# Hybrid DeltaNet and sparse-attention trunk: RMS norms whose reciprocal root is applied to the products, and reordered outer norms

## The chip, the cores and the metric

The kernel runs on one core of one Trainium2 chip. The metric is the device time of one execution in microseconds (us). Before the change it is 1827.06 us, the median of 3 runs (1824.49 to 1828.47).

## What is computed

Two decoder layers and a final norm on T = 320 tokens (256 of a prompt, 64 of eight sampled sequences) with D = 1024 features, in float32. Cut to what matters here:

```python
def rms_norm(x, w):
    xf = x.astype(jnp.float32)
    xf = xf * lax.rsqrt(jnp.mean(xf * xf, axis=-1, keepdims=True) + RMS_EPS)
    return xf.astype(x.dtype) * w
# gdn:  proj = rms_norm(x, norm_w) @ w_in; gated delta rule; x = x + o @ w_out
# ffn:  up = rms_norm(x, w) @ w_up; hidden = silu(conv(gate)) * up; x = x + hidden @ w_down
# nsa:  proj = rms_norm(x, norm_w) @ w_in; sparse attention; x = x + o @ w_out
# y = rms_norm(x, final_norm)
```

The order is gdn, ffn (first), nsa, ffn (second), final norm. The reciprocal root is one number per token, the weight one per feature.

## The kernel before

The tokens are kept turned: `xT` holds x as KD = 8 tiles of 128 features x 320 tokens. A projection is a row of *units*: gdn_in 24, gdn_out 8, ffn_up 22, ffn_down 8, nsa_in 10, nsa_out 4. A unit of gdn_in, ffn_up, nsa_in and nsa_out has two tiles of 128 output features, called lane 0 and lane 1 (in ffn_up the gate and the up half); a unit of the others has one, on lane 1. Each lane has two PSUM banks used in turn. For near-float32 results each operand is split in a high part and the rest, both in the rounded fp32r format: `high_part` on ScalarE (ACT, L496) and `low_part` on VectorE (DVE, L511) do this for the weights, and TensorE (PE) makes three products per tile (`three_products`, L535 to L537): 48 products for the two lanes of a unit with 8 feature tiles.

Weights arrive in a ring of RING = 4 slots, filled by SyncE's (SP) DMA queue in `stream`, which waits until PE is through with the unit that had the slot (`unit_done`). The engines run programs written out by hand for each stage and meet at barriers: each engine drains, raises `stage_closed` and waits until all four have.

A norm is made of these pieces. `square_tiles` (L363 to L367) lets ACT square each tile of x once the residual add of the stage before (`add_tile`, L1508, on DVE) has made it. `sum_of_squares` (L348 to L357) lets PE add them over features with 8 matmuls against a matrix of ones (L355). After a barrier `norm_stage` (L412 to L447) runs: ACT high part of unit 0, square root (L423), high part of unit 1; DVE low part of unit 0, reciprocal (L435), then for each of the 8 tiles the scaled x (L439), ACT's cast to the high part (L429) and DVE's low part (L444). PE then starts on unit 0. The start of the program has `pe_turns` (L369 to L383), which turns x, norm rows and convolution rows, and `copy_turned` (L385 to L400), which copies them out of PSUM and in between makes one square of all of x (L392). At the end `norm_stage` writes the normed x, `final_stage` (L2479 to L2510) turns it back in six groups, copies and stores it.

In `ffn_stage` (L1511) ACT takes the gate tile out of PSUM (L586, L587), makes the first tap of the convolution (L592), the next high part, silu (L615, L616) and the hidden high part (L1582); DVE makes the later taps (L610), the product of silu and up (L1619, which reads up from PSUM), the next low part and the hidden low part (L1623). PE also turns the last rows of each gate (L1556) into bank 4; ACT copies them out with `copy_rows` (L1586). In nsa_in ACT copies every tile out of PSUM, and POOL (GpSimd) issues loads in `pool_in`: attention tables, compressed keys `ckT` and values `cv`. In the rows stage POOL loads `w1_again` (L1896, 4 MB in two DMAs), which PE needs at L1831. The lines of such a program, as the second FFN's adds are:

```python
def add_tile(dve, name, j):
    dve.wait_ge(unit_done, UNITS[name][0] + j + 1)
    dve.tensor_tensor(xT[:, j, :], xT[:, j, :], bank(name, j, 1)[:, 0:T], ALU.add).then_inc(lane_free[1], 1)
```

## Time and profile before

| | |
|---|---|
| median of 3 runs | 1827.06 us |
| profiled execution | 1825.39 us, its span 1823.5 us |
| PE busy | 1638.0 us, 90% of the span |
| DVE busy | 865.5 us, 47% |
| ACT busy | 771.7 us, 42% |
| POOL busy | 195.6 us, 11% |
| DMA | 208.10 MB, mean 114 GB/s |
| gdn_in with its start, gates, core | 0 to 785 us |
| gdn_out, norm, ffn_up and ffn_down, first FFN | 785 to 1097 us |
| norm, nsa_in | 1097 to 1186 us |
| NSA rows, attention, nsa_out | 1186 to 1554 us |
| norm, second FFN | 1554 to 1802 us |
| final norm and stores | 1802 to 1823.5 us |

The page of the profile comes from one execution. Its share of busy time is a mean over stages of different kinds: where PE is the engine that never waits, work on other engines is free, and where PE idles, the chain that it waits for counts. So each boundary is looked at by itself, in the engines' timelines. PEclk is the clock that PE was granted, as a share of 2.4 GHz; 0.50 is 1.2 GHz.

### The profile page before, as it was taken

The numbers are of one execution on the slowest core, as the hardware profiler recorded it, in microseconds if no ns is written. First come the engines' busy times: TensorE is split into PE (matmuls) and PEld (weight loads), VectorE is DVE, ScalarE is ACT, GpSimd is POOL, SyncE is SP. The second block draws the span as 40 slices with busy tenths as digits, with TensorE's granted clock in tenths as the row PEclk, the third lists the DMA queues.
The fourth block names the chain that finished last, engine by engine and source line by source line (L and its number), as shares of the span: only waits on it lengthen the run. The fifth ranks groups of instructions, "written<-read, shape, count | busy, mean of one in ns | idle before, by whom it ended". The sixth has DMA issues, their size and how long they took to land. (4 is left out here: it accounts for less than half of the span.)

```text
span 1823.5 us, 37321 instructions
## 1 busy us (share of the span) xinstructions
PE 1638.0 (90%) x13536; PEld 1347.5 (74%) x13536; DVE 865.5 (47%) x1585; ACT 771.7 (42%) x1600; POOL 195.6 (11%) x396
## 2 busy tenths in 40 slices
PE   5999989999999999798999998977787777899997
PEld 4999756556655665487999997975555557799996
DVE  3875234444444344454555524224655543655632
ACT  3765233444234334433555414224444533555521
POOL 0331001011101110100000001021112100000000
PEclk7999979999989999888999998957778967999998
DMA  6445331321233122433555665344435313355640
GB/s 147 139 149 160 125 103 35 91 83 51 76 88 86 41 84 71 122 86 99 139 152 153 167 132 157 116 170 131 142 107 163 114 47 116 94 156 143 178 127 29
DMA packets 283161, 208.10 MB, mean 114 GB/s; under 512 B 29103, under 2 KB 274895, under 8 KB 282592
## 3 DMA queue, kind: packets, MB, share of 16 engines
q1 hardware_dynamic: 273750, 174.22, 34.2%
q0 software_dynamic: 9248, 31.80, 5.6%
q8 instruction: 79, 1.29, 0.3%
q14 instruction: 42, 0.34, 0.1%
q10 hardware_dynamic: 42, 0.44, 0.1%
HBM read 183.57 MB, written 22.85 MB: 113 GB/s over the span
## 5 line engine op out<-in xcount | busy, mean ns | idle before, releaser
L535 PE MATMUL psum<-h_rounded,weights_low 128*128 128x320 f32 x1248 | 395.5, 317 | 33.6 <-DVE h_low_ffn L444 16.7
L535 PEld LDWEIGHTS psum<-h_rounded,weights_low 128*128 128x128 f32 x1248 | 236.3, 189 | 40.2 <-issue 34.8
L997 PE MATMUL psum<-sbuf_resident 128*128 128x504 f32 x512 | 252.8, 609 | 0.0
L537 PE MATMUL psum<-h_rounded,weights_high_wide 128*128 128x320 f32 x704 | 220.2, 313 | 0.0
L536 PE MATMUL psum<-h_low_ffn,weights_high_wide 128*128 128x320 f32 x704 | 218.9, 311 | 0.0
L537 PE MATMUL psum<-h_rounded,weights_high 128*128 128x320 f32 x544 | 168.2, 309 | 0.0
L511 DVE TENSOR_TENSOR weights_low<-sbuf_resident,weights_high_wide 128x2048 fp32r<-128x2048 f32 (+1 forms) x60 | 149.8, 2499 | 16.5 <-ACT weights_high_wide L496 16.5
L610 DVE SCALAR_TENSOR_TENSOR sbuf_stages<-sbuf_stages,sbuf_resident 128x344 f32<-128x344 f32 (+1 forms) x184 | 105.5, 574 | 99.9 <-ACT sbuf_stages L592 96.1
L1030 ACT COPY sbuf_resident<-psum 64x256 f32<-64x256 f32 x256 | 93.8, 366 | 138.6 <-PE psum L990 136.0
L496 ACT CAST weights_high_wide<-sbuf_resident 128x2048 fp32r<-128x2048 f32 (+1 forms) x60 | 123.8, 2063 | 66.9 <-DMA sbuf_resident<-in_ffn_w_down_dram 60.1
L511 DVE TENSOR_TENSOR weights_low<-sbuf_resident,weights_high 128x2048 fp32r<-128x2048 f32 x46 | 105.3, 2293 | 74.5 <-ACT weights_high L496 74.5
L536 PEld LDWEIGHTS psum<-h_low_ffn,weights_high_wide 128*128 128x128 f32 x704 | 136.2, 194 | 0.0
L537 PEld LDWEIGHTS psum<-h_rounded,weights_high_wide 128*128 128x128 f32 x704 | 133.1, 189 | 0.0
L997 PEld LDWEIGHTS psum<-sbuf_resident 128*128 128x128 f32 x512 | 87.0, 194 | 54.1 <-issue 52.1
L536 PE MATMUL psum<-weights_low,weights_high 128*128 128x320 f32 x384 | 119.2, 310 | 0.0
L496 ACT CAST weights_high<-sbuf_resident 128x2048 fp32r<-128x2048 f32 x46 | 86.8, 1896 | 68.3 <-PE psum L537 36.9
L535 PE MATMUL psum<-hidden_high,weights_low 128*128 128x320 f32 x352 | 109.2, 310 | 0.0
L536 PE MATMUL psum<-hidden_low,weights_high_wide 128*128 128x320 f32 x352 | 108.9, 309 | 0.0
L537 PE MATMUL psum<-hidden_high,weights_high_wide 128*128 128x320 f32 x352 | 108.7, 309 | 0.0
L537 PEld LDWEIGHTS psum<-h_rounded,weights_high 128*128 128x128 f32 x544 | 104.2, 191 | 0.0
L586 ACT COPY sbuf_stages<-psum 128x256 f32<-128x256 f32 x76 | 28.3, 373 | 172.9 <-PE psum L537 171.1
L1508 DVE TENSOR_TENSOR sbuf_resident<-sbuf_resident,psum 128x320 f32<-128x320 f32 x24 | 11.7, 488 | 136.6 <-PE psum L537 136.6
(418 smaller groups left out, 3077.7 us busy)
## 6 DMA issues: line engine op xcount, KB each, us to landing
sbuf_resident<-in_ffn_w_up_dram SPq DMA_DIRECT2D x88, 512.0 KB, 4.8
sbuf_resident<-in_gdn_w_in_dram SPq DMA_DIRECT2D x48, 512.0 KB, 4.7
sbuf_resident<-in_ffn_w_down_dram SPq DMA_DIRECT2D x32, 704.0 KB, 5.8
sbuf_resident<-in_cache_nsa_kv_dram SPq DMA_DIRECT2D x256, 64.0 KB
sbuf_stages<-in_state_gdn_s_dram POOLq DMA_DIRECT2D x16, 512.0 KB, 5.5
out_gdn_s_sample_dram<-sbuf_stages SPq DMA_DIRECT2D x16, 512.0 KB, 3.7
sbuf_resident<-in_gdn_w_out_dram SPq DMA_DIRECT2D x16, 512.0 KB, 5.5
sbuf_stages<-in_cache_nsa_kv_dram POOLq DMA_DIRECT2D x64, 128.0 KB, 3.5
```

The source lines that it names most:

```text
L496: act.copy(dst[:, 0:kn * P], slot(w)[:, 0:kn * P]).then_inc(hi_done, 1)
L511: eng.tensor_tensor(ring_lo[w % RING][:, 0:kn * P], sl, hi[:, 0:kn * P], ALU.subtract).then_inc(lo_done, 1)
L535: pe.matmul(out, w_lo, x_hi_tile, start=first, stop=False)
L536: pe.matmul(out, w_hi, x_lo_tile, start=False, stop=False)
L537: return pe.matmul(out, w_hi, x_hi_tile, start=False, stop=last)
L586: act.copy(xp[:, hist:hist + TP], src[:, 0:TP])
L610: dve.scalar_tensor_tensor(out=y[:, 0:n_out], in0=xp[:, n:n + n_out], scalar=taps(n), in1=y[:, 0:n_out], op0=ALU.mult, op1=ALU.add).then_i ...
L997: last = pe.matmul(psum[:, H_BANK[t], 0:4 * NC2], w1[:, v, 8 * half + m, t * P:(t + 1) * P], blocks, start=(m == 0 and half == 0), stop=(m ...
L1030: last = act.copy(dst, src)
L1508: dve.tensor_tensor(xT[:, j, :], xT[:, j, :], bank(name, j, 1)[:, 0:T], ALU.add).then_inc(lane_free[1], 1)
```

## The change

The inner norms no longer make a normed x. During the residual adds of the stage before, ACT writes the high part of x times the weight and the squares, DVE the low part and the running sum of the squares. PE starts the next projection's lane 0 of unit 0 at once, then runs one ones-matmul on the sum, then lane 1. Root and reciprocal are made meanwhile, and the projections' results are multiplied by `rinv` where they leave PSUM: in ffn_up by `take_gate` and `take_up` on DVE (the product then reads SBUF twice), in nsa_in by DVE, which takes over all evictions from ACT; the 48 gate logits get an operation of their own. Six barriers become plain increments. High parts of ffn_up go to the narrow buffers. At the start unit 0's weights are loaded before the convolution rows, x is squared in three chunks of tokens, DVE adds the squares over tiles, one matmul sums them, and most turns come after it; there the normed x is still made. For the final norm, x times the weight is turned back in between the last down units, the sums come from three matmuls of one column, and the six copies to the output rows carry the reciprocal root. Because the final turns use bank 4, PE waits for ACT's last `copy_rows` ahead of the second ffn_down. The loads of `ckT` and `cv` move from nsa_in to the head of POOL's queue in the rows stage. The core of the diff:

```diff
+            for n in range(6):
+                turn(n)
+            pe.wait_ge(norm_rows_in, 16 * 4)
+            turn(6)
+            pe.wait_ge(dve_steps.sem, dve_steps.count("tile2"))
...
+            for c, cols in enumerate(CHUNKS):
+                copy_turn(act, 2 * c + 1)
+                act.wait_ge(dve_steps.sem, dve_steps.count(f"g{2 * c}"))
+                act.wait_ge(act_steps.sem, act_steps.count(f"g{2 * c + 1}"))
+                act.activation(hT[:, :, cols], xT[:, :, cols], ACT.Square).then_inc(act_steps.sem, act_steps.step(f"square{c}"))
+            act.wait_ge(S1["pe"].sem, S1["pe"].count("sum"))
+            act.activation(rinv, psum[:, SUM_BANK, 0:T], ACT.Sqrt, bias=eps_col, scale=1.0 / D).then_inc(act_steps.sem, act_steps.step("root"))
+            high_part(act, "gdn_in", 0, 0, KD * 2, free=True)
...
+            def dve_tile(self, dve, k):
+                dve.wait_ge(x_hi, SPLITS[self.units][0] + k + 1)
+                dve.scalar_tensor_tensor(out=self.low_rounded(k), in0=xT[:, k, :], scalar=self.weight(k), in1=hT_rounded[:, k, :],
+                                         op0=ALU.mult, op1=ALU.subtract).then_inc(x_lo, 1)
+                if k:
+                    self.add(dve, k)
...
+            def pe_sum(self, pe):
+                pe.wait_ge(self.dve_steps.sem, self.dve_steps.count(f"added{KD - 1}"))
+                pe.matmul(psum[:, SUM_BANK, 0:T], ones, rinv, start=True, stop=True).then_inc(self.pe_steps.sem, self.pe_steps.step("sum"))
...
+            def act_adding(self, act, kn):
+                n = UNITS[self.prev][1]
+                for j in range(n):
+                    if j + 3 < n:
+                        high_part(act, self.prev, 0, j + 3, kn)
+                    if self.units and j + 2 >= n:
+                        act.wait_ge(unit_done, UNITS[self.prev][0] + j + 1)
+                        high_part(act, self.units, 0, j + 2 - n, KD * 2)
+                    self.act_tile(act, j)
+
+            def dve_adding(self, dve, kn):
+                n = UNITS[self.prev][1]
+                for j in range(n):
+                    add_tile(dve, self.prev, j)
+                    if j + 3 < n:
+                        low_part(dve, self.prev, j + 3, kn)
+                    if j + 2 == n:
+                        low_part(dve, self.units, 0, KD * 2)
+                    self.dve_tile(dve, j)
+                low_part(dve, self.units, 1, KD * 2)
+
+            def pe_first_unit(self, pe, tile, high, low):
+                multiply_unit(pe, self.units, 0, 0, tile, high, low, KD, lanes=(0,), from_tile=0)
+                self.pe_sum(pe)
+                multiply_unit(pe, self.units, 0, 0, tile, high, low, KD, lanes=(1,))
...
+                    eng.wait_ge(rows_copied, len(ROWS) + 1)
+                    for j in range(8):
+                        multiply_unit(eng, down, 0, j, single_tile(NFT), lambda k: hidden_hi[:, k, :], lambda k: hidden_lo[:, k, :], NFT,
+                                      lanes=(1,), from_tile=NFT - 2 if j == 0 else None)
+                        if j:
+                            fin["pe_turn"](eng, j - 1)
...
                     eng.wait_ge(unit_done, product_count(up, 0, u, 1))
-                    eng.tensor_tensor(hid[:, u, :], sil[u % 2], bank(up, u, 1)[:, 0:T], ALU.mult).then_inc(lane_free[1], 1)
+                    eng.tensor_tensor(hid[:, u, :], bank(up, u, 1)[:, 0:T], rinv, ALU.mult).then_inc(lane_free[1], 1)
...
+                def take_gate(u):
+                    eng.wait_ge(half_done, product_count(up, 0, u, 0))
+                    if u >= 2:
+                        eng.wait_ge(tail_kept, u - 1)
+                    src, xp = bank(up, u, 0), xpf[u % 2]
+                    eng.tensor_tensor(xp[:, FP:FP + TP], src[:, 0:TP], rinv[:, 0:TP], ALU.mult)
+                    eng.tensor_tensor(padded(xp, FP)[:, :, FP:FP + TQ], seqs(src[:, TP:T]), seqs(rinv[:, TP:T]), ALU.mult).then_inc(lane_free[0], 1)
...
-                            ins_ = act.copy(kvT[:, 2 * (n - 4) + l, :], src)
...
+                            ins_ = dve.tensor_tensor(kvT[:, 2 * (n - 4) + l, :], src, rinv, ALU.mult)
                         ins_.then_inc(lane_free[l], 1)
-
...
+                dve.tensor_tensor(gates48, psum[0:48, 6, 0:T], rinv[0:48, :], ALU.mult).then_inc(gate_scaled, 1)
...
+                pool.dma_start(ckT, ck_dram).then_inc(cmp_in, 16)
+                pool.dma_start(cv, cv_dram).then_inc(cmp_in, 16)
...
+            def pe_turn(pe, k):
+                pe.wait_ge(x_hi, SPLITS["final"][0] + k + 1)
+                for tb in range(3):
+                    last = pe.transpose(psum[:, Y_BANK[2 * tb + k // 4], (k % 4) * P:(k % 4 + 1) * P], hT[:, k, y_rows[tb]], ident)
+                last.then_inc(s["pe"].sem, s["pe"].step(f"x{k}"))
...
-            sums_f0["pe"](pe)
-            pe.drain().then_inc(stage_closed, 1)
-            pe.wait_ge(stage_closed, 4 * 5)
+            pe.sem_inc(stage_closed, 1)
```

**DVE between gdn_out and the first ffn_up.** Before, from the last three residual adds (L1508): low part of unit 0, reciprocal, then scale and low part of each tile (the first of eight).

```order
L1508 TENSOR_TENSOR sbuf_resident<-sbuf_resident,psum 128x320 x3
L511 TENSOR_TENSOR weights_low_49<-sbuf_resident,weights_high_wide_57 128x2048
L435 RECIPROCAL sbuf_resident<-sbuf_resident 128x320
L439 SCALAR_TENSOR_TENSOR sbuf_stages<-sbuf_resident 128x320 x2
L444 SCALAR_TENSOR_TENSOR h_low_ffn_66<-sbuf_stages,h_rounded 128x320
L439 SCALAR_TENSOR_TENSOR sbuf_stages<-sbuf_resident 128x320
```

Of the change, from the last residual add (L1592) on: L488 is the low part of the weighted x, L479 the running sum, L597 low parts of weights, L1720 and L1721 the gate's eviction, L1713 the up half's.

```order
L1592 TENSOR_TENSOR sbuf_resident<-sbuf_resident,psum 128x320
L488 SCALAR_TENSOR_TENSOR weighted_x_low<-sbuf_resident,h_rounded 128x320
L479 TENSOR_TENSOR sbuf_resident<-sbuf_resident,sbuf_stages 128x320
L597 TENSOR_TENSOR weights_low_50<-sbuf_resident,weights_high_54 128x2048
L503 RECIPROCAL sbuf_resident<-sbuf_resident 128x320
L1720 TENSOR_TENSOR sbuf_stages<-psum,sbuf_resident 128x256
L1721 TENSOR_TENSOR sbuf_stages<-psum,sbuf_resident 128x8x8
L696 SCALAR_TENSOR_TENSOR sbuf_stages<-sbuf_stages,sbuf_resident 128x336 x2
L597 TENSOR_TENSOR weights_low_51<-sbuf_resident,weights_high_55 128x2048
L1713 TENSOR_TENSOR sbuf_stages<-psum,sbuf_resident 128x320
```

The work on the eight tiles has moved ahead of the last add, low part 0 lies before the rows shown, and the reciprocal has only the low part of unit 1 ahead of it and the first eviction behind it.

**PE between the second ffn_up and ffn_down,** before, with what each row waits for (L1556 turns the last rows of a gate):

```order
L537 MATMUL psum<-h_rounded,weights_high_wide_58 128x320
L1556 MATMUL psum<-sbuf_resident,sbuf_stages 18x128 [waits ffn1_rows_copied,ffn1_tail_kept]
L1556 MATMUL psum<-sbuf_resident,sbuf_stages 18x128 [waits ffn1_tail_kept]
L1502 UNCONDITIONAL_BRANCH [waits activations_low_part_done]
L535 MATMUL psum<-hidden_high,weights_low_51 128x320 [waits lane1_banks_free,weights_low_part_done]
```

and of the change (L1640 is that turn, L621 and L622 the products):

```order
L623 MATMUL psum<-h_rounded,weights_high_54 128x320
L1640 MATMUL psum<-sbuf_resident,sbuf_stages 18x128 [waits ffn1_rows_copied,ffn1_tail_kept]
L1640 MATMUL psum<-sbuf_resident,sbuf_stages 18x128 [waits ffn1_tail_kept]
L621 MATMUL psum<-hidden_high,weights_low_51 128x320 [waits lane1_banks_free,weights_low_part_done,ffn1_rows_copied]
L622 MATMUL psum<-hidden_low,weights_high_wide_59 128x320
```

The first down product has one more wait, `ffn1_rows_copied`.

**ACT at the same place,** before, from the last hidden high part:

```order
L1582 CAST hidden_high<-sbuf_stages 128x320 [waits lane1_banks_free]
L496 CAST weights_high_wide_60<-sbuf_resident 128x2816 [waits weights_in_slot3]
L1586 COPY sbuf_resident<-psum 18x256 [waits ffn1_tails_turned]
L496 CAST weights_high_wide_57<-sbuf_resident 128x2816 [waits unit_done,weights_in_slot0]
L496 CAST weights_high_wide_58<-sbuf_resident 128x2816 [waits unit_done,weights_in_slot1]
```

and of the change:

```order
L1674 CAST hidden_high<-sbuf_stages 128x320 [waits ffn1_product]
L582 CAST weights_high_wide_60<-sbuf_resident 128x2816 [waits weights_in_slot3]
L1678 COPY sbuf_resident<-psum 18x256 [waits ffn1_tails_turned]
L582 CAST weights_high_wide_57<-sbuf_resident 128x2816 [waits unit_done,weights_in_slot0]
L582 CAST weights_high_wide_58<-sbuf_resident 128x2816 [waits unit_done,weights_in_slot1]
L2669 ACTIVATE sbuf_resident<-sbuf_resident 128x320 [waits lane1_banks_free]
L472 ACTIVATE sbuf_resident<-sbuf_resident 128x320
```

The copy for which PE now waits (L1586, now L1678) keeps its place behind one wide cast; behind it the weighted copies and squares (L2669, L472) come in among the casts.

## Rows read from the trace of the kernel before

**Rows 1.** Windows: stretch, length, busy (count) by engine, PEclk, DMA share, GB/s

```profile
846.00:866.00 20.00, 11.81 (x52) 9.76 (x51) 14.35 (x21) 9.79 (x16) 1.68 (x4) 0.74 0.19 53
...
1576.00:1723.00 147.00, 147.00 (x1003) 145.86 (x1002) 87.10 (x104) 79.86 (x153) 9.61 (x62) 1.00 0.57 154
...
1802.00:1823.00 21.00, 8.51 (x38) 6.66 (x36) 8.01 (x12) 3.80 (x6) 1.64 (x3) 0.72 0.18 63
```

**Rows 2.** PE timeline, the first FFN's norm: start us, duration us, instruction

```profile
844.83 4.48 PE L355 MATMUL psum<-sbuf_resident 128*128 128x320 f32 x16
...
857.50 0.60 PE L535 MATMUL psum<-h_rounded,weights_low 128*128 128x320 f32 x1 [8.19 <-DVE h_low_ffn L444]
...
867.34 0.31 PE L535 MATMUL psum<-h_rounded,weights_low 128*128 128x320 f32 x1
```

**Rows 3.** PE timeline at the start of the program

```profile
8.59 4.39 PE L382 MATMUL psum<-sbuf_resident,sbuf_stages 128*128 128x128 f32 x24 [8.59 <-DMA sbuf_resident<-tables_dram]
...
47.12 0.31 PE L535 MATMUL psum<-h_rounded,weights_low 128*128 128x320 f32 x1
```

**Rows 4.** ACT timeline at the start

```profile
13.49 2.34 ACT L392 ACTIVATE sbuf_resident<-sbuf_resident 128x2560 f32<-128x2560 f32 x1
...
41.83 0.46 ACT L429 CAST h_rounded<-sbuf_resident 128x320 fp32r<-128x320 f32 x1 [0.41 <-DVE sbuf_resident L439]
```

**Rows 5.** ACT timeline in the NSA norm

```profile
1102.95 1.28 ACT L423 ACT_TABLE_LOAD   x1
1104.25 0.53 ACT L423 ACTIVATE sbuf_resident<-psum,sbuf_stages 128x320 f32<-128x320 f32 x1
```

**Rows 6.** DVE timeline in the first FFN's norm

```profile
853.60 2.15 DVE L435 RECIPROCAL sbuf_resident<-sbuf_resident 128x320 f32<-128x320 f32 x1
```

**Rows 7.** DVE timeline, one round of the first FFN's up-projection

```profile
917.68 0.49 DVE L1619 TENSOR_TENSOR sbuf_stages<-sbuf_stages,psum 128x320 f32<-128x320 f32 x1 [1.07 <-ACT sbuf_stages L616]
918.09 2.29 DVE L511 TENSOR_TENSOR weights_low<-sbuf_resident,weights_high_wide 128x2048 fp32r<-128x2048 f32 x1
920.29 0.48 DVE L1623 SCALAR_TENSOR_TENSOR hidden_low<-sbuf_stages,hidden_high 128x320 fp32r<-128x320 f32 x1
```

**Rows 8.** DVE timeline at the start

```profile
35.43 1.01 DVE L439 SCALAR_TENSOR_TENSOR sbuf_resident<-sbuf_resident 128x320 f32<-128x320 f32 x2
```

**Rows 9.** ACT timeline, the same round as rows 7

```profile
914.30 0.37 ACT L586 COPY sbuf_stages<-psum 128x256 f32<-128x256 f32 x1 [3.50 <-PE psum L537]
...
914.82 0.58 ACT L592 ACTIVATE sbuf_stages<-sbuf_stages,sbuf_resident 128x336 f32<-128x336 f32 x1
...
915.30 1.89 ACT L496 CAST weights_high_wide<-sbuf_resident 128x2048 fp32r<-128x2048 f32 x1
...
917.41 0.24 ACT L616 ACTIVATE sbuf_stages<-sbuf_stages 128x64 f32<-128x64 f32 x1
...
921.49 0.37 ACT L586 COPY sbuf_stages<-psum 128x256 f32<-128x256 f32 x1 [3.49 <-PE psum L537]
```

**Rows 10.** PE timeline, start of the NSA rows stage

```profile
1185.26 4.15 PE L1798 MATMUL psum<-sbuf_resident,sbuf_stages 128*128 128x128 f32 x36
...
1201.89 1.32 PE L1831 MATMUL psum<-sbuf_stages,sbuf_resident 128*128 128x60 f32 x5 [4.58 <-DMA sbuf_stages<-in_nsa_cmp_w_dram]
```

**Rows 11.** Windows, two short stretches

```profile
1318.00:1324.00 6.00, 4.67 (x32) 3.67 (x33) 2.74 (x7) 4.42 (x12) 0.00 (x0) 0.72 0.52 167
1198.00:1200.00 2.00, 0.00 (x0) 0.00 (x0) 1.84 (x7) 0.00 (x0) 0.00 (x0) 0.50 1.00 342
```

**Rows 12.** PE timeline at the second FFN's first down unit

```profile
1723.14 0.39 PE L535 MATMUL psum<-hidden_high,weights_low 128*128 128x320 f32 x1
```

**Rows 13.** ACT timeline at the same place

```profile
1726.67 0.35 ACT L1586 COPY sbuf_resident<-psum 18x256 f32<-18x256 f32 x1
```

**Rows 14.** PE timeline, final norm

```profile
1801.05 4.49 PE L355 MATMUL psum<-sbuf_resident 128*128 128x320 f32 x16
```

**Rows 15.** POOL timeline, the last store

```profile
1819.77 0.54 POOL L2507 DMA_DIRECT2D out_y_sample_dram<-sbuf_stages  x1 [0.72 <-ACT sbuf_stages L2497]
```

509 lines of the change are left out of this document (275 added, 234 removed).

## The prediction, made before the changed kernel ran

> **What bounds the kernel now.** I read the view by time windows first. In the FFN up-projection from 1576 to 1723 us TensorE (PE) is busy all the time: 1003 matmuls in 147.00 us, so one 128x320 product takes 0.147 us at the full clock of 2.4 GHz [rows 1]. A stretch around a norm looks otherwise: from 846 to 866 us PE is busy 11.81 of 20 us at a granted clock of 0.74, and from 1802 us to the end 8.51 of 21 us [rows 1]. PE's timeline gives the length of one boundary. The last product of the stage before is followed at 844.83 us by the ones-matmuls of the norm; the first product of the next stage starts at 857.50 and that of its unit 1 at 867.34; what the first one waited for, 8.19 us, is named behind it: the low part of the normed x [rows 2]. From the end of one stage's products to unit 1 of the next it is 22.51 us, of which the 48 products of unit 0 need 48 x 0.147 = 7.06. PE is the pace in the wide projections, and in the norms the chain sum, root, reciprocal, scale, cast, low part. The two boundaries before nsa_in and ffn_up1 have the same length and the same kinds of step.
>
> **The start.** The turns of x end at 8.59 + 4.39 = 12.98 [rows 3]. Before, one Square of 2560 columns follows, 2.34 us [rows 4]. In its place stand squares by token chunk (the last has 512 columns, by the same rate 0.6 us), three DVE adds (0.4 to 0.9 each) and one ones-matmul, 0.9 at the low clock: the sum is there at 17.4. Root 0.53 [rows 5], reciprocal 2.15 [rows 6] and the low part of unit 0's weights, 2.29 [rows 7], follow in series: 22.3. The eight tiles take from 35.43 [rows 8] to the last cast's end at 42.29 [rows 4], 6.86; after that stands a copy and a turn that PE waits for, 0.8. PE starts the products at 30.0. Unit 0 begins at the low clock after such a wait, as the one that took from 857.50 to 867.34, 9.84 [rows 2], so unit 1 starts at 39.8, where it was 47.12 [rows 3]. **-7.3**, bounds 3 and 10: what I can't see is when x and 1 MB of weights, now ahead of the conv rows, land.
>
> **Three boundaries.** ACT now makes x times weight (the high part) and its square, DVE the low part and a running sum, while PE is still in the units before. Only tile 7 is left when PE ends. An add is 0.49, a weighted copy and a low part 0.5 each; with starts 0.41 apart where two DVE operations follow each other [rows 7], tile 7's low part is ready 3.15 after PE ends. PE has 21 products (3.1 us) of lane 0 before it needs that tile. The sum's one matmul costs 0.28 and stands behind lane 0, when the last add (3.5) is through. So unit 1 starts 7.45 after, not 22.51: **-15.06 each, -45.2 for three**. The cover of root and reciprocal: the root ends at 4.8, DVE goes on with low part 1 until 5.65 and the reciprocal until 7.8, the first eviction ends at 8.4, and PE wants that bank back only for unit 2 at 14.65. Low part 2 is ready at 13.1. Silu's table load, 1.28 as the one of the root [rows 5], delays low part 3 to 20.9, needed at 21.85. The smallest slack is some 0.6 us; if it is gone, each FFN start loses its excess. Bounds for the three: -46 and -38.
> The row says that after a table load of 1.28 at 1102.95 the activation starts at 1104.25, 0.02 later [rows 5]. The Trainium skill ("ScalarE: Activation LUTs", What ACT_TABLE_LOAD costs) adds a drain of about 1380 ns, 2.66 us for each switch; by that low part 3 comes 0.4 us late at each FFN start, and the sum would be about 0.9 us less gain.
>
> **The FFN round.** DVE gets two multiplications more per unit (gate and up leave PSUM through it), ACT loses two copies. Before, PE's round is 921.49 - 914.30 = 7.19 [rows 9]. The new round goes through both engines. From the gate's eviction start: 0.56 for its two pieces (ACT's pair took 0.52 [rows 9]); then as before from the first tap at 914.82 to silu's end at 917.41 + 0.24, 2.83 [rows 9]; product, low part of the weights, hidden low and take_up at 0.41, 2.20, 0.40 and 0.41 from start to start [rows 7]. With small handovers the next gate can start at 6.87, below 7.19: DVE's work is hidden behind PE, at **0**. What it costs without that cover is rival A.
> DVE's product ran 0.49 us from 917.68, and the next operation started at 918.09, 0.41 later [rows 7]. The Trainium skill ("VectorE: DVE Perf Modes", The DRAIN you can't avoid) has the next operation wait until the pipeline is empty; by that the round is that of rival A.
>
> **The NSA stages.** Evictions go from ACT to DVE, 20 x 0.49 in 68 us, hidden; scaling the gates after the last product adds **+0.45** before the barrier. The loads of compressed keys and values, 1.008 MB, now stand on POOL's queue ahead of the w1 weights, for which PE waited until 1201.89 [rows 10]. At 342 GB/s [rows 11] they take 2.9: **+3.0**. Bounds: 0 if they slip in beside other waits, 6 if they go at half that rate.
>
> **Down-projection of the second FFN.** PE now waits there for the last copy of rows (L1586) before its first product, since the transposes take those banks. PE went on at 1723.14 [rows 12] while that copy ended at 1726.67 + 0.35 [rows 13], behind a wide cast. The wait is 3.9, and 0.4 for take_up on the way: 4.3. After gaps of that length the clock goes low: from 1318 to 1324, after an idle gap of 4.26, it was granted 0.72 [rows 11], a mean between 1.2 and 2.4 GHz that costs 1.7. **+6.0**, bounds 3.5 and 8.
>
> **The end.** 24 transposes go in among the down products, 4.15 / 36 = 0.115 each [rows 10]; 18 of them are in the way: **+2.0**. After the last product the chain before was 1801.05 [rows 14] to the end of the span at 1823.5, 22.45. Now: add .49, weighted copy .57, square .47, add .45, three small matmuls, root and reciprocal of 3 columns some 1.0, three evictions of 128x512 in turn some 1.8: 4.8. Two stores stand ahead of the last on POOL, 0.54 each with their waits as now [rows 15], so it is issued at about 6.4; the last one took from 1819.77 [rows 15] to the end at 1823.5, 3.73. About 10.1, bounds 9.7 and 12: **-12.35**.
>
> **Sum:** -7.3 - 45.2 + 0 + 0.45 + 3.0 + 6.0 + 2.0 - 12.35 = -53.4. The profiled execution took 1825.39 and would take 1772.0; the median is 1.67 above it, so I forecast 1827.06 - 53.4 = **1773.7 us**. With every term at its good end it would be 1764, with every one at its bad end 1792.
>
> **Rivals.**
> A. DVE and ACT become the pace of the FFN up-projection. For it: the new round has only 0.3 us of room, and it goes back and forth between two engines six times. Against: starts 0.41 apart [rows 7]. With whole durations added up (gate pieces .64 by estimate, tap .58, ACT's high part 1.89, silu .65, two handovers .06 [rows 9], product .49, low part 2.29, hidden low .48, take_up .49 [rows 7]) the round is 7.58: PE loses 0.38 in each of 20 rounds, less the 1.3 that the two banks buffer, in two FFNs: +12.6, so 1786. At a round of 7.9 it is +26, 1799.
> B. Slower than before, by the same place: the product now reads two SBUF operands and every round has two more semaphore hops with PSUM reads. If each round takes over 8.6 us (2 x (20 x 1.4 - 1.3) = 53.4), the gain is used up. At 9.0 us it is 1827 - 53.4 + 69.4 = 1843. Nothing in the rows makes 1.7 us of two operations of 0.49, so it gets little.
> C. The root's chain is not covered: unit 2 or 3 of a projection stalls, since DVE has low parts 1 and 2, the reciprocal and the evictions all in 14 us. Each boundary loses 2 to 3 us, 1781.
> D. Less is lost than I count: PE's wait at the second down-projection costs 3.5, the loads slip in, the start gains 10: 1764 to 1768, and to 1762 where the end of the program is shorter as well.
> E. The change does nothing, since what the norms gave is lost in waits on low parts (the ring's slots come free only as fast as before, and SP's queue is the pace). Against: the DMA share is 0.57 in the busiest long stretch [rows 1]. 1825 to 1829.
>
> **Chances.** Forecast 0.58, A 0.16, C 0.13, D 0.08, E 0.02, B 0.03. A measurement of this kernel tells about 0.2% (3.7 us) from no change. Faster 0.95, same 0.02, slower 0.03. The range takes the forecast's own bounds, C, most of D and two thirds of A: 1763 to 1796.
>
> **What would show it.** In the changed profile: from the last product of gdn_out, ffn_down0 and nsa_out to unit 1 of the next stage 7.4 to 8.5 us, with a granted clock of 1.0 in between; the first product at 30 us; in ffn_up a PE that is busy all the time with rounds of 7.2 us, and DVE's next gate eviction starting as PE ends its lane 0, not later; an idle gap of some 4 us on PE ahead of the second down-projection, ended by ACT's copy of rows; PE's wait for w1 some 3 us longer; 10 us from the last product to the end. The prediction is wrong if PE waits in ffn_up rounds for lane banks (then A), or if the DVE round is above 7.2. It is wrong as a whole if the first unit 1s start more than 10 us after the stage before.

## Result

The changed kernel takes 1761.41 us in the median of 4 runs (1756.73 to 1772.79), beside 1825.78 for the kernel before (4 runs, 1824.07 to 1828.47). The ratio is 0.9697, with a 95% interval of 0.9653 to 0.9741: 3.0% faster (the two medians alone would give 0.965). Two later comparisons, on two different chips, gave 0.9712 (0.9663 to 0.9761) and 0.9710 (0.9664 to 0.9756), with the changed kernel at 1764.37 us beside 1818.73, and at 1767.1 beside 1820.8. In the last one a run of 1782.31 us counts as slow and stays out of the ratio, and without it the median is 1766.44 us. The forecast was 1773.7 us, 53.4 less than before and a ratio of 0.971, in a range of 1763 to 1796. The ratio agrees with the forecast; the first median lies 1.6 us under the range, the two later ones lie in it. In medians the change is worth 64.4, 54.4 and 54.4 us.

The profiled execution took 1756.73 us, its span 1755.1, against 1825.39 and 1823.5: 68.4 us less in the span, 15 more than forecast; it is also the fastest of the first four runs. From its page, the first line of part 1:

```profile
PE 1592.0 (91%) x13470; PEld 1318.9 (75%) x13470; DVE 913.7 (52%) x1741; ACT 746.8 (43%) x1504; POOL 190.0 (11%) x396
```

The time windows (start:end, length, busy us and count of PE, PE's weight loads, DVE, ACT and POOL, then PEclk, DMA share, GB/s) that correspond to [rows 1]: the first FFN's boundary, the second up-projection and the end; then the start of the second ffn_down.

```profile
834.00:854.00 20.00, 20.00 (x136) 19.56 (x135) 13.07 (x17) 9.85 (x11) 0.92 (x6) 1.00 0.56 155
...
1508.00:1655.00 147.00, 147.00 (x1006) 145.93 (x1006) 106.62 (x165) 68.97 (x109) 9.57 (x62) 1.00 0.58 155
...
1734.00:1755.00 21.00, 11.35 (x79) 10.86 (x77) 3.98 (x8) 5.24 (x9) 1.64 (x3) 0.85 0.19 63
...
1661.00:1667.00 6.00, 5.83 (x22) 5.83 (x23) 5.97 (x2) 5.00 (x3) 1.03 (x2) 0.51 0.46 85
```

The boundary has no idle PE and a clock of 1.00, where PE had been busy 11.81 of 20 us at 0.74. The up-projection is as full as before, with DVE at 106.6 of 147 us instead of 87.1. PE's timeline (start, duration, instruction, count) across the boundary corresponds to [rows 2]:

```profile
834.06 0.31 PE L623 MATMUL psum<-gated_high,weights_high 128*128 128x320 f32 x1
...
834.21 0.31 PE L621 MATMUL psum<-h_rounded,weights_low 128*128 128x320 f32 x1
...
837.95 0.70 PE L495 MATMUL psum<-sbuf_resident 128*128 128x320 f32 x2
...
841.57 0.31 PE L621 MATMUL psum<-h_rounded,weights_low 128*128 128x320 f32 x1
```

The new stage's first product starts 0.15 us after the last one of gdn_out, the sum's matmul stands behind lane 0, and unit 1 begins at 841.57, 7.36 us after the stage before (7.45 was forecast; its own terms, 7.06 of products and 0.28 for the sum, give 7.34). DVE's timeline in that boundary and in rounds of the up-projection, early and late ones:

```profile
834.41 0.49 DVE L1592 TENSOR_TENSOR sbuf_resident<-sbuf_resident,psum 128x320 f32<-128x320 f32 x1 [1.98 <-PE psum L623]
...
836.80 0.55 DVE L488 SCALAR_TENSOR_TENSOR weighted_x_low<-sbuf_resident,h_rounded 128x320 fp32r<-128x320 f32 x1 [1.91 <-ACT h_rounded L483]
...
837.67 2.28 DVE L597 TENSOR_TENSOR weights_low<-sbuf_resident,weights_high 128x2048 fp32r<-128x2048 f32 x1
...
839.88 2.15 DVE L503 RECIPROCAL sbuf_resident<-sbuf_resident 128x320 f32<-128x320 f32 x1
...
842.16 0.42 DVE L1720 TENSOR_TENSOR sbuf_stages<-psum,sbuf_resident 128x256 f32<-128x256 f32 x1
...
889.92 0.41 DVE L1720 TENSOR_TENSOR sbuf_stages<-psum,sbuf_resident 128x256 f32<-128x256 f32 x1
...
893.37 0.49 DVE L1709 TENSOR_TENSOR sbuf_stages<-sbuf_stages 128x320 f32<-128x320 f32 x1 [1.08 <-ACT sbuf_stages L702]
...
893.78 2.28 DVE L597 TENSOR_TENSOR weights_low<-sbuf_resident,weights_high 128x2048 fp32r<-128x2048 f32 x1
...
896.78 0.41 DVE L1720 TENSOR_TENSOR sbuf_stages<-psum,sbuf_resident 128x256 f32<-128x256 f32 x1
...
924.84 0.42 DVE L1720 TENSOR_TENSOR sbuf_stages<-psum,sbuf_resident 128x256 f32<-128x256 f32 x1 [0.25 <-PE psum L623]
...
932.04 0.43 DVE L1720 TENSOR_TENSOR sbuf_stages<-psum,sbuf_resident 128x256 f32<-128x256 f32 x1 [0.25 <-PE psum L623]
```

The last add, tile 7's low part, low part 1, the reciprocal and the first gate eviction stand as summed (low part ready at 3.15 after PE's last product: 837.35 - 834.21 = 3.14). From one gate eviction to the next it is 896.78 - 889.92 = **6.86 us**, where 6.87 was forecast [rows 7, 9], and PE's rounds stay at 7.20 in the mean. The 6.86 can be seen only because DVE enters the projection late: its third gate eviction starts 2.8 us after the moment that rounds of 7.20, counted back from the later ones, would give. It catches up in eight rounds of 6.86; from then on it waits 0.25 us for PE in each, as at 924.84 and 932.04.

PE at the second ffn_down and ACT at the same place correspond to [rows 12, 13]; behind them PE in the NSA rows stage [rows 10], the first products of the program [rows 3], and POOL's last stores [rows 15]:

```profile
1655.40 0.38 PE L1640 MATMUL psum<-sbuf_resident,sbuf_stages 128*18 128x128 f32 x2
1661.17 0.64 PE L621 MATMUL psum<-hidden_high,weights_low 128*128 128x320 f32 x1 [5.39 <-ACT sbuf_resident L1678]
1660.76 0.36 ACT L1678 COPY sbuf_resident<-psum 18x256 f32<-18x256 f32 x1
```

```profile
1166.04 2.17 PE L1942 MATMUL psum<-sbuf_stages,sbuf_resident 128*128 128x60 f32 x9 [6.07 <-DMA sbuf_stages<-in_nsa_cmp_w_dram]
...
29.36 0.62 PE L621 MATMUL psum<-h_rounded,weights_low 128*128 128x320 f32 x1
...
1748.61 1.17 POOL L2656 DMA_DIRECT2D out_y_prompt_dram<-sbuf_stages  x2 [86.17 <-ACT sbuf_stages L2633]
...
1749.86 0.54 POOL L2658 DMA_DIRECT2D out_y_sample_dram<-sbuf_stages  x1
```

Stage by stage, from PE's timeline in both traces (first and last product of each):

| stretch | before | after | difference | forecast |
|---|---|---|---|---|
| start to the end of gdn_in | 218.09 | 210.11 | -8.0 | -7.3 |
| gates, core, gate norm, gdn_out | 626.6 | 624.0 | -2.6 | 0 |
| three boundaries with the projection behind each | 435.6 | 391.5 | -44.1 | -45.2 |
| first ffn_down, its wait and products | 78.1 | 79.2 | +1.1 | 0 |
| NSA rows stage up to w1 products | 17.1 | 19.4 | +2.3 | +3.45 |
| w1 products and attention, up to nsa_out | 317.1 | 301.1 | **-16.0** | 0 |
| nsa_out | 30.4 | 30.1 | -0.3 | 0 |
| second ffn_down, its wait and products | 78.1 | 88.2 | +10.2 | +8.0 |
| from the last product to the end | 22.6 | 11.6 | -11.0 | -12.35 |

The stretches with a forecast term and the first ffn_down sum to -49.5 here, against -53.4. The other -18.9 us are in three stretches that were put at 0. The one large difference is in the attention stage, where the change touches nothing but one wait at its start, on loads issued well before.

### The profile page after: what moved, and what is told of

Read it like the earlier page. It is cut to its first block and busy times, and to the rows that moved or that the text cites. A ratio compares the mean times of both kernels' runs of the same rounds, so it can differ in the third digit from the quotient of the medians.

```text
span 1755.1 us, 37259 instructions
## 1 busy us (share of the span) xinstructions
PE 1592.0 (91%) x13470; PEld 1318.9 (75%) x13470; DVE 913.7 (52%) x1741; ACT 746.8 (43%) x1504; POOL 190.0 (11%) x396
## 5 line engine op out<-in xcount | busy, mean ns | idle before, releaser
L621 PE MATMUL psum<-h_rounded,weights_low 128*128 128x320 f32 x1248 | 391.4, 314 | 0.0
L623 PE MATMUL psum<-h_rounded,weights_high 128*128 128x320 f32 x1248 | 386.7, 310 | 0.0
L622 PE MATMUL psum<-weighted_x_low,weights_high 128*128 128x320 f32 x864 | 266.3, 308 | 0.0
L621 PEld LDWEIGHTS psum<-h_rounded,weights_low 128*128 128x128 f32 x1248 | 235.1, 188 | 3.0 <-DVE weighted_x_low L488 0.5
L623 PEld LDWEIGHTS psum<-h_rounded,weights_high 128*128 128x128 f32 x1248 | 234.7, 188 | 0.0
L597 DVE TENSOR_TENSOR weights_low<-sbuf_resident,weights_high 128x2048 fp32r<-128x2048 f32 x90 | 205.7, 2287 | 50.9 <-ACT weights_high L582 50.9
L582 ACT CAST weights_high<-sbuf_resident 128x2048 fp32r<-128x2048 f32 x90 | 169.9, 1893 | 91.7 <-PE psum L623 69.7
L622 PEld LDWEIGHTS psum<-weighted_x_low,weights_high 128*128 128x128 f32 x864 | 165.3, 191 | 0.2
L622 PE MATMUL psum<-weights_low,weights_high 128*128 128x320 f32 x384 | 119.2, 310 | 0.0
L621 PE MATMUL psum<-hidden_high,weights_low 128*128 128x320 f32 x352 | 110.9, 315 | 6.3 <-ACT sbuf_resident L1678 5.4
L678 ACT ACTIVATE sbuf_stages<-sbuf_stages,sbuf_resident 128x336 f32<-128x336 f32 (+1 forms) x76 | 44.1, 581 | 164.6 <-DVE sbuf_stages L1721 163.5
L622 PE MATMUL psum<-hidden_low,weights_high_wide 128*128 128x320 f32 x352 | 110.0, 313 | 0.0
L622 PEld LDWEIGHTS psum<-weights_low,weights_high 128*128 128x128 f32 x384 | 73.8, 192 | 0.0
L1592 DVE TENSOR_TENSOR sbuf_resident<-sbuf_resident,psum 128x320 f32<-128x320 f32 x24 | 11.7, 487 | 119.1 <-PE psum L623 119.1
L621 PEld LDWEIGHTS psum<-hidden_high,weights_low 128*128 128x128 f32 x352 | 67.3, 191 | 6.8 <-ACT sbuf_resident L1678 5.7
L622 PEld LDWEIGHTS psum<-hidden_low,weights_high_wide 128*128 128x128 f32 x352 | 67.1, 191 | 0.0
```

What stands on the lines that cost most here:

```text
L582: act.copy(dst[:, 0:kn * P], slot(w)[:, 0:kn * P]).then_inc(hi_done, 1)
L597: eng.tensor_tensor(ring_lo[w % RING][:, 0:kn * P], sl, hi[:, 0:kn * P], ALU.subtract).then_inc(lo_done, 1)
L621: pe.matmul(out, w_lo, x_hi_tile, start=first, stop=False)
L622: pe.matmul(out, w_hi, x_lo_tile, start=False, stop=False)
L623: return pe.matmul(out, w_hi, x_hi_tile, start=False, stop=last)
L678: return act.activation(y[:, 0:n_out], xp[:, 0:n_out], ACT.Copy, scale=tap)
```

## Experiments

What was open: whether the 16 us of the attention stage belong to the change; what of a boundary's 15 us is the overlap of the root; how much room the FFN round has; what the wait at the second ffn_down, the early weights and the stores are worth. Times by stretch are from each run's profile, medians from its timed runs beside the kernel before on the same chip.

**The attention stage.** First the kernel before, with the two loads moved alone:

```diff
 def pool_in(pool):
-                pool.dma_start(ckT, ck_dram).then_inc(att_in, 16)
-                pool.dma_start(cv, cv_dram).then_inc(att_in, 16)
...
 def pool_rows(pool):
+                pool.dma_start(ckT, ck_dram).then_inc(cmp_in, 16)
+                pool.dma_start(cv, cv_dram).then_inc(cmp_in, 16)
...
+                pool.wait_ge(cmp_in, 32)
```

> The kernel before with only the loads of ckT and cv moved to the head of POOL's queue in the rows stage. My theory: PE's wait for the w1 weights becomes 2.3 to 3.0 us longer, as in the changed kernel, and nothing else changes; the attention stage takes 317 us from PE's first w1 product to nsa_out as before, so the kernel is at 1829 to 1830. Rival: the order of these loads is what made the attention stage 16 us shorter (317 to 301 us) in the changed kernel; then this kernel is at about 1813.

It took 1825.09 us beside 1815.39, ratio 1.0039 (1.0011 to 1.0067). From nsa_in's last product to the first w1 product it is 19.94 us instead of 17.05, +2.9 as expected, and the attention stage took 314.0 us. So the loads cost 2.9 us, and the rival, 1813 us, is excluded. The ratio is a loss of 2 to 12 us; what of it lies beyond these 2.9 the runs can't tell. Then the changed kernel as it is, beside other kernels:

> The changed kernel once more, unchanged, beside the others on this chip. My theory on the 16 us that its attention stage gained beyond the forecast: the work there is the same, and only the moments at which TensorE's clock falls and rises differ from execution to execution. Then this kernel takes 301 to 317 us from PE's first w1 product to nsa_out, not again 301, and its runs and those of the kernel before both spread over some 15 us. Rival: the changed loads made the stage shorter; then it is 301 us again, within 2.

1764.37 us (1758.23 to 1772.66); the stage took 306.6 us, not 301.1. And the kernel before with all that follows nsa_in moved later:

```diff
             project(pe)
+            for _ in range(14):
+                pe.matmul(psum[:, SUM_BANK, 0:T], ones, xT[:, 0, :], start=True, stop=True)
```

> The kernel before with 14 useless ones-matmuls on PE after nsa_in, which makes all that follows start some 8 us later (a call takes 0.56 us) and changes nothing else. My theory (the attention stage's time depends on when the clock falls): its own 317 us move to any value from 300 to 317, with the granted clock of its rounds between 0.74 and 0.94, and the kernel is 8 us slower with a scatter of 10 us. Rival: the stage is fixed by its code, and takes 314 to 317 us as in both profiles of this code so far; then the kernel is slower by 8 us within 2.

1826.32 us beside 1819.39, ratio 1.0043 (1.0014 to 1.0072); the stretch ahead of the stage grew by 7.7 us, and the stage took only 308.6. So the same code took 317.1 us in one execution and 308.6 in another. Whether the moved start did that, or it would have differed anyway, one execution of each doesn't show. The time windows of the stage, PEclk behind the busy times, of the kernel before, the changed one, its second run, e3 (below), e6, and the changed one's third run:

```profile
1202.00:1519.00 317.00, 241.31 (x2449) 182.21 (x2449) 151.00 (x379) 131.88 (x371) 39.92 (x71) 0.75 0.36 116
```

```profile
1166.00:1467.00 301.00, 221.42 (x2448) 168.98 (x2448) 150.46 (x379) 132.90 (x372) 37.48 (x68) 0.82 0.39 124
```

```profile
1163.00:1470.00 307.00, 232.36 (x2448) 176.54 (x2448) 151.16 (x379) 132.51 (x372) 38.06 (x69) 0.78 0.38 122
```

```profile
1181.00:1494.00 313.00, 240.59 (x2448) 181.94 (x2448) 150.75 (x379) 132.14 (x372) 37.50 (x68) 0.75 0.37 119
```

```profile
1210.00:1519.00 309.00, 234.17 (x2449) 176.69 (x2450) 151.11 (x379) 133.80 (x372) 40.41 (x72) 0.78 0.37 119
```

```profile
1174.00:1492.00 318.00, 242.84 (x2448) 184.09 (x2447) 150.57 (x378) 133.21 (x372) 36.95 (x67) 0.74 0.36 117
```

In all of them PE has 2448 or 2449 matmuls, but its busy time goes from 221.4 to 242.8 us as the granted clock goes from 0.82 to 0.74, and the stage from 301 to 318 us. What is left of each window when PE's busy time is taken off is 72 to 80 us, without a trend: the spread is in the time of the matmuls, as a lower clock makes it. The stage is 301.1, 306.6, 305.2, 313.1, 310.1, 311.0 and 313.5 us in the profiles of the changed code and its variants (changed, again, e1, e3, e4, e8, e9) and 317.1, 314.0 and 308.6 in those of the code before. The two groups overlap, so no cause in the change is needed; the means differ by 4.5 us, which can't be told from chance with ten profiles. The changed kernel's third profile, of its run of 1782.31 us, has 318.6 us here, more than any of the code before. The stretch from gdn_in to the end of gdn_out scatters too: 619.4 to 632.1 us in the profiles of the changed code, 626.6 to 627.4 in those of the code before. The kernel before scattered as much over the chips: 1824.07 to 1828.47 in the first 4 runs, but 1804.38 to 1827.17 in later ones. And the changed one, once more:

> The changed kernel a third time, on the same chip as e12, for the comparison. My theory: 1757 to 1772 us for its runs as before, median 1761 to 1767, and an attention stage between 300 and 317 us. Rival, if the clock depends on the chip more than on the moment: all its runs within 4 us of each other.

1767.1 us in the median of 6, from 1753.88 to 1782.31, where 1757 to 1772 was expected; five of the six lie between 1753.88 and 1772.06, so the rival, all within 4 us, is excluded; the stage's 318.6 us lie just outside the expected 300 to 317. The Trainium skill ("TensorE: Matmul & The Clock Gate", Part 1: The HAM clock gate) says that one kernel shows different numbers of slow matmuls at its start from run to run, and puts the ramp penalty under 1% of a typical span. These traces show such differences between executions of one kernel in the middle of it too; as to the size, this one stage moved by 16 us, 0.9% of the span.

**The overlap of the root.** PE waits for the sum and the reciprocal before unit 0; the work on the tiles stays early. With it the 21 products that had covered the work on tile 7 move behind the wait as well:

```diff
             def pe_first_unit(self, pe, tile, high, low):
-                multiply_unit(pe, self.units, 0, 0, tile, high, low, KD, lanes=(0,), from_tile=0)
                 self.pe_sum(pe)
+                pe.wait_ge(self.dve_steps.sem, self.dve_steps.count("inverse"))
+                multiply_unit(pe, self.units, 0, 0, tile, high, low, KD, lanes=(0,), from_tile=0)
```

> The changed kernel, in which PE waits at each of the three inner norms for the reciprocal before unit 0, so that the early work on the tiles is kept and only the overlap of root and reciprocal with the products is lost. My theory: PE starts unit 0 7.8 us after the end of the last products (low part of tile 7 and last add to 3.5, sum 0.3, root 0.5, reciprocal behind low part 1, to 7.8), and some 2 us are lost at half clock behind that gap: 9.5 to 10.5 us for each, 29 to 31 us in all. Rival: PE had slack elsewhere, or the stages behind take the loss up; then under 20 us.

1792.79 us, ratio 0.9885 (0.9846 to 0.9924). PE's gaps at the three boundaries are 8.01, 8.02 and 6.81 us instead of 0.15, and the projections behind them 2.0, 0.9 and 2.2 us longer, at half clock in their first products: 27.4 us in all by the stretches, a little under the 29 to 31 expected and well over the rival's 20. PE in the first of them, and DVE's reciprocal:

```profile
834.29 1.43 PE L495 MATMUL psum<-sbuf_resident 128*128 128x320 f32 x2 [3.44 <-DVE sbuf_resident L479]
...
838.55 0.64 PE L622 MATMUL psum<-h_rounded,weights_low 128*128 128x320 f32 x1 [2.83 <-DVE sbuf_resident L503]
836.35 2.15 DVE L503 RECIPROCAL sbuf_resident<-sbuf_resident 128x320 f32<-128x320 f32 x1
```

The gap has two parts. The last product of gdn_out starts at 830.54, and up to the sum at 834.29 PE waits for tile 7 and the last add: 3.7 us. Sum, root and reciprocal take the other 4.3, to 838.55. Only these 4.3 are the overlap of the root. So of the 12.7 us that a gap lost in the changed kernel, some 4.3 are sum, root and reciprocal, now beside the products, 3.6 are the work on tile 7, also beside them, and the other 4.8 are the tiles made early, the barrier and the eight ones-matmuls; the clock comes on top.

**The room in the FFN round.**

```diff
                 def take_up(u):
                     eng.wait_ge(unit_done, product_count(up, 0, u, 1))
+                    for b_ in (6, 7):
+                        eng.tensor_tensor(psum[:, b_, 0:T], bank(up, u, 1)[:, 0:T], rinv, ALU.mult)
                     eng.tensor_tensor(hid[:, u, :], bank(up, u, 1)[:, 0:T], rinv, ALU.mult).then_inc(lane_free[1], 1)
```

> The changed kernel with two more multiplications of 128x320 on DVE in every round of ffn_up, written to unused PSUM banks, so the round of DVE and ACT grows from the measured 6.86 by 2 x 0.40 to 7.66 us, 0.46 over PE's 7.20. My theory: PE starts to wait in the rounds, 20 x 0.46 less what the banks buffer (1.3 to 2) for each of two FFNs, 14 to 17 us in all. Rival: the round of 6.86 has hidden slack (ACT's part overlaps more when DVE is late), and the loss is under 5 us; or successive DVE operations do not overlap when the engine is full, and the loss is above 25 us.

1793.89 us, ratio 0.9882 (0.9834 to 0.993). My 14 to 17 us were too few: by the stretches it lost 15.7 and 13.9 us, 29.5 in all. DVE's rounds, and PE at the end of the first up-projection:

```profile
882.05 0.42 DVE L1722 TENSOR_TENSOR sbuf_stages<-psum,sbuf_resident 128x256 f32<-128x256 f32 x1
...
889.71 0.42 DVE L1722 TENSOR_TENSOR sbuf_stages<-psum,sbuf_resident 128x256 f32<-128x256 f32 x1
```

```profile
1006.96 0.28 PE L1640 MATMUL psum<-sbuf_resident,sbuf_stages 128*18 128x128 f32 x1 [4.02 <-POOL sbuf_stages L687]
...
1009.49 0.61 PE L621 MATMUL psum<-hidden_high,weights_low 128*128 128x320 f32 x1 [2.25 <-DVE hidden_low L1727]
```

The round is 889.71 - 882.05 = 7.66 us, just 6.86 + 0.80, so successive operations start less than a duration apart also where the chain through DVE and ACT is the pace. (DVE itself is not full in it: it waits 1.7 us of each round for ACT.) The up-projection lost 7.8 us, as my sum has it (20 x 0.46 less what the banks hold back). But what the banks hold back is not saved: ffn_down needs the last round's result, and PE waits 6.96 us there instead of 1.40, with 2.2 us of half clock behind. The 13.4 us of 7.8 and 5.6 are more than 22 x 0.46 = 10.1: DVE's late start of 2.8 us, which the changed kernel makes up for in rounds of 6.86, is not made up for in rounds of 7.66. The rival's threshold of 25 us was passed for another reason than it gave.

**The wait at the second ffn_down.** Without the long wait PE needs one on the hidden low parts of all but the last two tiles, which is put in:

```diff
-                    eng.wait_ge(rows_copied, len(ROWS) + 1)
+                    eng.wait_ge(x_lo, SPLITS[down][0] + NFT - 2)
                     for j in range(8):
...
+                        if j == 1:
+                            eng.wait_ge(rows_copied, len(ROWS) + 1)
                         if j:
                             fin["pe_turn"](eng, j - 1)
```

> The changed kernel with one wait moved: PE waits for ACT's last copy of rows ahead of the first turn into bank 4 (after the second down unit), not ahead of the first down product. My theory: the wait of 5.66 us at the second ffn_down shrinks to the 1.4 us that the first FFN has at the same place, and the 22 products at half clock behind it (0.27 instead of 0.147 us each) go as well: the second down-projection starts 4.3 us earlier and is 2.1 to 2.7 us shorter, some 6.5 us in all. Rival: the wait is only a symptom, PE waits next for the low part of the first down weights, which ACT's wide casts hold up; then under 2 us.

1752.95 us, ratio 0.9661 (0.9618 to 0.9703). PE there:

```profile
1661.13 0.38 PE L1640 MATMUL psum<-sbuf_resident,sbuf_stages 128*18 128x128 f32 x2
1662.10 0.41 PE L621 MATMUL psum<-hidden_high,weights_low 128*128 128x320 f32 x1 [0.59 <-DVE hidden_low L1727]
```

The gap from the last product is 1.12 us, from 5.91, and the second ffn_down 79.8 us instead of 82.3: 7.3 us, where 6.5 was expected. What it has over the 77.8 of before are 21 turns at 0.1 us each.

**The start.** Unit 0's weights at their former place in SP's queue:

```diff
-            stream(sp, "gdn_in", pair_source(ins["gdn_w_in"][0]), only=0)
...
             sp.dma_start(w_ab, ins["gdn_w_in"][0].rearrange("(k p) n -> p k n", p=P)[:, :, CONV_CH + V_DIM:]).then_inc(small_in, 16)
+            stream(sp, "gdn_in", pair_source(ins["gdn_w_in"][0]), only=0)
```

> The changed kernel with the 1 MB of unit 0's weights loaded at their former place, behind the convolution rows and small tables. My theory: the high part of unit 0 started at 17.43 us, behind the root and not behind its load, and the low part at 19.64, so there is little room: the weights now land after 20 us, since the rows ahead took until about 23 us in the changed kernel, and PE's first product moves from 29.4 to 33 to 36 us, +4 to +7 us. Rival: the weights landed long before, and the chain of squares and tiles alone sets the start; then within 1 us.

1774.26 us beside the changed kernel's 1764.37, ratio 0.9741 (0.9685 to 0.9798). ACT's high part of unit 0, in the changed kernel and in this one:

```profile
17.43 1.89 ACT L582 CAST weights_high<-sbuf_resident 128x2048 fp32r<-128x2048 f32 x1
```

```profile
24.01 1.90 ACT L582 CAST weights_high<-sbuf_resident 128x2048 fp32r<-128x2048 f32 x1 [5.83 <-DMA sbuf_resident<-in_gdn_w_in_dram]
```

It waits 5.83 us for the load, and PE's first product comes at 35.8 us instead of 29.4. That is in the 4 to 7 us expected. Of the 8 us that the start gained, 6.4 hang on the weights being first in the queue; the reordered squares alone would have waited for them.

**The end.** The wait moved as above, and the stores issued by SP:

```diff
             def pool(eng):
+                eng.wait_ge(y_stored, 16 * 3)
+
+            def sp(eng):
                 v = outs["y_prompt"].rearrange("b (t p) d -> p (b t) d", p=P)
...
+            fin["sp"](sp)
```

> The changed kernel with the moved wait of e1_wait_at_turns and with the three last stores issued by SP instead of POOL. The last store was issued 6.4 us after the last product as forecast, but took 5.2 us, since three were issued within 1.3 us. My theory: from the last product of the second ffn_down to the end of the span it takes 11.6 us in the changed kernel; SP issues each store as its evictions end, so the last is issued 0.5 to 1 us earlier and the end is 1 to 2 us nearer: 9.6 to 10.6 us. Rival: the stores' transfer sets the end, not the issue; then 11 to 11.6 us.

1756.53 us beside 1764.37, ratio 0.9645 (0.9606 to 0.9685). From the last product to the end it takes 10.44 us instead of 11.57, within the 9.6 to 10.6 expected. In the changed kernel three stores are issued within 1.3 us and the last takes 5.2 us (1749.86 to 1755.1); in the kernel before it was issued 1.3 us behind the second and 2.9 behind the first and took 3.73 [rows 15]. SP issues the last store half a microsecond earlier, and it lands 4.55 us after that: of the 1.1 us, 0.5 are the issue and 0.6 the store itself, which neither theory nor rival had. That the store takes longer because the other two are still moving is not shown.

**The clock in the rows stage.** Calls of no use keep PE busy in two waits (one call shows as two matmuls in the views, so 12 calls are x24):

```diff
+                for _ in range(8):
+                    pe.matmul(psum[:, 6, 0:T], ones, rinv, start=True, stop=True)
                 pe.wait_ge(dve_steps.sem, dve_steps.count("gate"))
...
+                for _ in range(12):
+                    pe.matmul(psum[:, 6, 0:T], ones, rinv, start=True, stop=True)
                 pe.wait_ge(w1_again_in, 32)
```

> The changed kernel with ones-matmuls of no use (8 and 12 calls of 128x320 into a free bank) in PE's two waits of the NSA rows stage, 4.8 and 6.1 us long, after which it ran 27.7 us of w1 products at half clock (granted clock 0.50). My theory: the low clock is left over from these waits; with PE busy it stays at 1.0 and the w1 products take 14 to 20 us instead of 27.7, so the stage is 8 to 14 us shorter. Rival: the small products themselves (60 columns) do not hold the clock up; then it falls to 0.50 within them and they take over 24 us, and the kernel is within 3 us of the changed one.

1750.19 us beside 1764.37, ratio 0.9633 (0.9587 to 0.9679). The w1 products (L1942 in the changed kernel, L1946 here): a time window and PE's timeline, first of the changed kernel:

```profile
1166.00:1170.00 4.00, 3.96 (x19) 3.96 (x19) 0.00 (x0) 0.00 (x0) 1.91 (x4) 0.50 1.06 398
...
1179.74 13.86 PE L1942 MATMUL psum<-sbuf_stages 128*128 128x60 f32 x64
```

```profile
1166.00:1180.00 14.00, 14.00 (x120) 13.52 (x119) 0.00 (x0) 0.52 (x2) 2.08 (x4) 1.00 0.68 231
...
1159.17 8.42 PE L1920 MATMUL psum<-sbuf_resident 128*128 128x320 f32 x24
1167.43 7.25 PE L1946 MATMUL psum<-sbuf_stages,sbuf_resident 128*128 128x60 f32 x64
1174.52 7.31 PE L1946 MATMUL psum<-sbuf_stages 128*128 128x60 f32 x64
```

They took 7.25 + 7.31 us at a granted clock of 1.00 instead of 13.91 + 13.86 at 0.50; from the first start to the last end that is 14.4 us instead of 27.6. All findings together, with one more place:

```diff
             def pe_out(pe):
+                for _ in range(12):
+                    pe.matmul(psum[:, SUM_BANK, 0:T], ones, rinv, start=True, stop=True)
```

> Everything that the runs so far point to, in the changed kernel: the wait on the rows' copy moved to the turns, the last stores issued by SP, useless ones-matmuls in PE's waits in the NSA rows stage (8 and 10 calls) and ahead of nsa_out (12 calls in a wait of 10 us). My theory: the terms are in different places and add up: 7.2 for the moved wait, 1.1 for the stores, 12 to 14 for the w1 products at full clock, 2 to 3 for the first products of nsa_out at full clock: 22 to 25 us below the changed kernel's 1764 on this kind of chip, 1739 to 1742, with the attention stage spread over some 10 us. Rival: a clock kept high in one place is lost in another, or the calls outlast the waits, and less than 12 us are left.

1743.18 us (1738.26 to 1747.79), ratio 0.9585 (0.9552 to 0.9618). It is just above the expected 1739 to 1742, beside a kernel before at 1819.39 on this chip. The moved wait (7.4 us), the stores (1.1) and nsa_out (27.7 us instead of 30.1) are there in its profile, but its w1 products ran slow again (PE's timeline, and a time window):

```profile
1161.14 5.66 PE L1922 MATMUL psum<-sbuf_resident 128*128 128x320 f32 x20
1168.48 12.47 PE L1948 MATMUL psum<-sbuf_stages,sbuf_resident 128*128 128x60 f32 x64 [1.69 <-DMA sbuf_stages<-in_nsa_cmp_w_dram]
1180.75 13.86 PE L1948 MATMUL psum<-sbuf_stages 128*128 128x60 f32 x64
...
1170.00:1174.00 4.00, 4.00 (x22) 4.00 (x21) 0.00 (x0) 0.00 (x0) 0.13 (x1) 0.51 1.05 310
```

The 10 calls ended at 1166.8, PE waited 1.69 us, and the clock, still 1.00 up to 1170, was 0.51 in the next 4 us, with PE busy in the products. The profiled execution is the slowest of the six, 1747.79 us; whether the clock was lost here in the others can't be seen. With 13 calls:

> The kernel of e11 with 13 calls ahead of the w1 products instead of 10. In e11 the 10 calls ended 1.7 us before the weights landed, and the w1 products took 12.5 + 13.9 us, as at half clock; in e10, where the calls ran on until after the landing, they took 7.3 + 7.3. My theory: even a wait of 1.7 us ahead of these small products is enough to lose the clock in them; with 13 calls PE goes straight from the calls to the products, which take under 16 us in all, and the kernel is 9 to 12 us below e11's 1743. Rival: e10 had the clock by chance, as the attention stage has; then the products take over 24 us again, and the kernel stays at 1741 to 1745.

```profile
1154.14 8.60 PE L1922 MATMUL psum<-sbuf_resident 128*128 128x320 f32 x26
1162.57 7.25 PE L1948 MATMUL psum<-sbuf_stages,sbuf_resident 128*128 128x60 f32 x64
1169.65 7.31 PE L1948 MATMUL psum<-sbuf_stages 128*128 128x60 f32 x64
```

They take 14.4 us again, as was expected before the run. With e10 and e12 on one side and e11 on the other that speaks for the gap as the cause, with one profiled execution of each. The median is 1741.02 us (1729.73 to 1750.33), ratio 0.9586 (0.9538 to 0.9633): 25 us below the changed kernel on the same chip, but only 2 below e11, not 9 to 12, and by the ratio to before not below it at all. In its profile the stage up to nsa_out, w1 products included, took 296.2 us where e11's took 300.2: of the 11.7 us that the products gained, 7.7 were lost again in the rest of it, and the 13 calls, which outlast the load, made the stretch ahead of the products 1.4 longer. Whether the 7.7 are the same scatter of the clock or an early high clock costs one later stays open.

## Why the prediction was right

The measured ratio, 0.970 to 0.971, agrees with the forecast's 0.971, and the steps that carry it, the boundaries, the start and the end, came out as summed. That it agrees so closely is in part luck: the terms measure -49.5 in all, four less than forecast, and the medians of -54.4 have the rest from stretches that I put at 0. Two of the three medians lie in rival D's 1764 to 1768, but D's conditions did not hold (the wait cost more than counted, not less); on those chips the kernel before was itself at 1818.73 and 1820.8 us. By its steps:

- **Three boundaries, -45.2:** -44.1 measured. Tile 7's low part and the place of the sum were right to 0.1 us, and nothing behind them waited; rival C did not come true. By e3 a boundary's 12.7 us of gap are 4.3 of sum, root and reciprocal and 8.4 of work on the tiles, barrier and ones-matmuls.
- **FFN round, 0:** the round of 6.86 us is the one summed from starts 0.41 apart. Rival A needed whole durations, which the Trainium skill's rule ("VectorE: DVE Perf Modes", The DRAIN you can't avoid) would give; neither the changed kernel nor e4, where the round through DVE is the pace, shows it. The same section lets a next operation that is not held start earlier, which would fit these rows; the prediction left that out. Rival A's price was too low, though: e4 shows that what the banks hold back is lost in the stage behind, which waits for the last round. An estimate from e4, 29.5 x 0.38 / 0.46, puts a round of 7.58 at some 24 us and not 12.6.
- **Silu's table load:** silu starts 0.01 us after the load ends, without the drain of about 1.38 us that the Trainium skill ("ScalarE: Activation LUTs", What ACT_TABLE_LOAD costs) adds, and PE does not wait:

```profile
850.74 1.28 ACT L701 ACT_TABLE_LOAD   x1
852.03 0.42 ACT L701 ACTIVATE sbuf_stages<-sbuf_stages 128x256 f32<-128x256 f32 x1
```

- **Start, -7.3:** -8.0. e8 shows that the part I could not see, when the weights land, decides 6.4 of them.
- **Loads, +3.0 and gates, +0.45:** +2.3 together; e2 has the loads alone at +2.9, so the 0.45 of the gates can't be seen.
- **Second ffn_down, +6.0 and turns, +2.0:** +10.2 together. The gap grew by 5.6 us, not 4.3, the half clock behind it cost 2.5 (82.3 us less e1's 79.8), not 1.7, and the turns the 2.0. I had left out that DVE and ACT finish the last round 1.1 us later, which PE waits for in the first FFN as well; that is the term of 0 that measured +1.1.
- **The end, -12.35:** -11.0. The last store was issued 6.4 us after the last product, as summed; its own 3.73 us were mis-sized: with three stores within 1.3 us it took 5.2.
- **The profiled execution, -53.4:** -68.4, and this is where the forecast was off: I took one profiled execution for a fixed yardstick. 16 us of its gain are in the attention stage, whose time goes with its clock; with no change in the code it was 301.1, 306.6 and 318.6 us in the changed kernel's three profiles. The medians of the first comparison, 64.4 us apart, lean the same way.

## What to carry over

Where a norm's factor is one number per token, multiply it in where results leave PSUM and let the matmuls start on the unnormed operand; then count the new round on the evicting engine from start to start, and remember that the stage behind it waits for its last round, and that a late start is only made up for while the engine's round is shorter than the pace. Before crediting a difference in a stage that the change doesn't touch, repeat the run: here that difference was 16 us. Moving a wait from the start of a stage to the first use of the buffer that it guards was worth 7 us.
